# Down projections of a two-block transformer kernel: high and low activation parts moved as one 512-column matmul, the halves added at evacuation

## The chip, the core and the metric

The kernel runs on one NeuronCore of one Trainium2 chip. The metric is the device time of one execution in microseconds; the kernel before has a median of 1790.25 us over three runs.

## What is computed

256 tokens of width 1024 pass through two blocks. The first has a feed-forward network (FFN) before and after a token mixer; the second has two layers of the same shape. That makes six FFNs, numbered 0 to 5, and three mixers. Each FFN is

```
def swiglu(x, w_gate, w_up, w_down):
    return (jax.nn.silu(x @ w_gate) * (x @ w_up)) @ w_down
h = h + FFN_RES * g1[:, None, :] * swiglu(u, w_ff1_gate[l], w_ff1_up[l], w_ff1_down[l])
...
x = x + 0.5 * swiglu_2(rms_norm(x, ffn1_norm[l]), ffn1_w_in[l], ffn1_w_out[l])
```

with a hidden width of 2816. The change concerns `@ w_down` and the residual addition behind it, in all six FFNs.

## The kernel before

All activations lie transposed: features on the 128 partitions, the 256 tokens (`T`) in the free dimension, so the residual `h` is 8 tiles (`KD`) of 128x256 and the hidden activation 22 tiles (`KF`). Every large product is made in three float32r matmuls: weight and activation are each split into a high part (rounded to fp32r) and a low part (the rest), and high x high, high x low and low x high are accumulated (`three`, L1487 to L1491). ScalarE makes `whi` from the loaded weights `raw` (L717), VectorE makes `wlo` = raw - whi (L957). Weights come in chunks through a ring of 4 slots (`RING`): SyncE loads a slot when `lo_ready` says that VectorE has used it, ScalarE splits three chunks ahead (`HI_LEAD`), VectorE two chunks ahead (`LO_LEAD`), and TensorE counts `chunk_used`.

A down projection walks over m, the 8 output tiles. Each m has two chunks, an even one (t = 2m) with hidden tiles 0 to 10 and an odd one (t = 2m + 1) with hidden tiles 11 to 21. A chunk is 11 calls of `three`, which is 33 matmuls of 256 columns, each with a weight load of its own (a high weight tile is loaded twice, for its two matmuls). The sum lies in the first 256 columns of one of two PSUM banks (`acc`, "bank" in the profile), used in turn.

VectorE works through its part in a written order. `down(t)` for an even t is one weight split; for an odd t it is, in this order: wait for `chunk_used`; the evacuation L1121 (h = bank * gate + h, which signals `evacuated`); in FFNs 1 to 4 `gained_lo` (L986), which makes the low part of the next stage's input and waits for ScalarE's high part of the same tile (L743), which in turn waits for `evacuated`; and a weight split. FFNs 0 and 5 have no `gained_lo`. In FFN 0 VectorE also does two `ada_sum` steps per m (L1056: a modulation matrix, streamed in by GpSimd's queue, times the condition vector). GpSimd squares each finished tile of `h` for the next norm (L553, L554). VectorE, ScalarE and TensorE run most of a down projection in a hardware loop of two m per turn; VectorE's last turn is unrolled in FFNs 1 to 5, and all of it in FFN 0. The rows of `order` in the section on the change mark where an instruction waits.

Of the kernel before, what the change touches and what calls it, by code (L numbers as in the profile page):

```python
# [17 lines left out]
F32R = mybir.dt.float32r  # L18
U8 = mybir.dt.uint8
ALU = mybir.AluOpType  # L20
# [3 lines left out]
P = 128  # L24
T = 256
TT = T // P
D = 1024
KD = D // P
F = 2816
KF = F // P  # L30
# [130 lines left out]
def build(nc, a, out):  # L161
    with ExitStack() as ctx:
        ctx.enter_context(nc.allow_non_contiguous_dma(reason="two vectors of a few elements"))
        def sb(name, shape, dt=F32):
            return ctx.enter_context(nc.sbuf_tensor(name, shape, dt))

        def sem(name):
            return ctx.enter_context(nc.semaphore(name))
# [9 lines left out]
        wlo = sb("wlo", [P, RING, SLOT], F32R)  # L178
        h = sb("h", [P, KD, T])
        u = sb("u", [P, KD, T])  # L180
        uhi = sb("uhi", [P, KD, T], F32R)
        ulo = sb("ulo", [P, KD, T], F32R)
        work = sb("work", [P, 4, T])
        silu, hid = work[:, 0:2], work[:, 2:4]
        gate_up = work[:].rearrange("p (a b) t -> p a b t", a=2)
# [46 lines left out]
        qk_sq = toe  # L232

        hidden = ExitStack()
        hhi = hidden.enter_context(nc.sbuf_tensor("hhi", [P, KF, T], F32R))
        hlo = hidden.enter_context(nc.sbuf_tensor("hlo", [P, KF, T], F32R))
        hidden.close()
        lv = sb("lv", [P, TT, 512])
        place_of_aq_ak = ExitStack()
# [24 lines left out]
        acc = psum[0:2]  # L264
# [15 lines left out]
        evacuated = sem("evacuated")  # L280
        silu_ready = sem("silu_ready")
        hid_ready = sem("hid_ready")
        hhi_ready = sem("hhi_ready")
        hlo_ready = sem("hlo_ready")
        ada_landed = [sem(f"ada_landed{i}") for i in range(2)]
# [110 lines left out]
        def tiles_of(tile, m, it=0, per=0):  # L396

            if isinstance(it, int):
                return tile[:, m]
            return tile[:, bass.ds(it * per + m, 1)].rearrange("p a t -> p (a t)")  # L400
# [4 lines left out]
        def residual_gate(i):  # L405

            return [half[:, 0:8], half[:, 8:16]][i] if i < 2 else half8

        def seg(name):
            return FIRST[name], UNIT[name]  # L410
# [540 lines left out]
        def _(dve):  # L951
# [19 lines left out]
            def split_ahead(n, it=0):  # L971
                if n + LO_LEAD < len(COLS):
                    split_lo(n + LO_LEAD, it)
# [29 lines left out]
            def by_token(n):  # L1003
                return rstd[:, 0:T].unsqueeze(1).to_broadcast([P, n, T])
# [70 lines left out]
            def ffn(i):  # L1075
                n0, e0 = seg(f"up{i}")

                def step(t, it=0):
                    g = it * RING + KF * i + t + 1
                    ps = acc[(e0 + t) % 2]  # L1080
                    if i < 2:
                        dve.wait_ge(silu_ready, g)
                        nc.vector.tensor_tensor(hid[:, t % 2], silu[:, t % 2], ps[:, T:2 * T], ALU.mult  # L1083
                                                ).then_inc(evacuated, 1)
                        split_ahead(n0 + t, it)
                        if i == 0:
                            ada_sum(2 + t, it)
                    else:

                        pair = gate_up[:, t % 2]  # L1090
                        dve.wait_ge(chunk_used, it * RING + RING + n0 + t + 1)
                        nc.vector.tensor_tensor(pair, ps[:].rearrange("p (a t) -> p a t", a=2), by_token(2), ALU.mult  # L1092
                                                ).then_inc(evacuated, 1)
                        split_ahead(n0 + t, it)
                        dve.wait_ge(silu_ready, g)
                        nc.vector.tensor_tensor(pair[:, 1], pair[:, 0], pair[:, 1], ALU.mult).then_inc(hid_ready, 1)
                    dve.wait_ge(hhi_ready, g)
                    src = hid[:, t % 2] if i < 2 else gate_up[:, t % 2, 1]
                    nc.vector.tensor_tensor(tiles_of(hlo, t, it, RING), src, tiles_of(hhi, t, it, RING).bitcast(F32),  # L1099
                                            ALU.subtract).then_inc(hlo_ready, 1)  # L1100

                up_turns(dve, i, step)
                if i == 0:
                    dve.wait_ge(mod_taken, 1)
                    link(nc.vector.tensor_scalar(half[:, 0:8], mod[:, 2 * KD:3 * KD], 0.5, None, ALU.mult))
                n0, e0 = seg(f"down{i}")
                g = residual_gate(i)
                after = next_gain(f"down{i}")
                if i == 2:
                    final_residual()  # L1110

                def down(t, it=0):
                    if t % 2 == 0:
                        split_ahead(n0 + t, it)
                        if i == 0:
                            ada_sum(2 + KF + t, it)
                    else:
                        m = t // 2
                        dve.wait_ge(chunk_used, it * RING + RING + n0 + t + 1)
                        gm, hm = column(g, m, it, 2), tiles_of(h, m, it, 2)  # L1120
                        nc.vector.scalar_tensor_tensor(out=hm, in0=acc[(e0 + m) % 2][:, 0:T], scalar=gm, in1=hm,  # L1121
                                                       op0=ALU.mult, op1=ALU.add).then_inc(evacuated, 1)
                        if after is not None:
                            gained_lo(SPLITS.index(FOLLOWS[f"down{i}"]), after, m, it, 2)
                        split_ahead(n0 + t, it)
                        if i == 0:
                            ada_sum(2 + KF + t, it)


                turns = 2 * KD // RING - 1 if i else 0  # L1130
                if turns:
                    with dve.Fori(0, turns) as it:
                        for t in range(RING):
                            down(t, it)
                for t in range(turns * RING, 2 * KD):
                    down(t)
# [267 lines left out]
            ins = nc.vector.tensor_copy(vec_b[:, 0:B_ROWS], ps_score[:, P:P + B_ROWS])  # L1404
# [79 lines left out]
        def _(pe):  # L1484
            mm = nc.tensor.matmul

            def three(dst, wh, wl, xh, xl, first, last):  # L1487

                mm(dst, wh, xh, start=first, stop=False)  # L1489
                mm(dst, wh, xl, start=False, stop=False)  # L1490
                return mm(dst, wl, xh, start=False, stop=last)  # L1491

            def chunk_in(n, it=0):
                pe.wait_ge(lo_ready, it * RING + RING + n + 1)

# [62 lines left out]
            def ffn(i, stats=None):  # L1558

                n0, e0 = seg(f"up{i}")  # L1560
                waits = KD * SPLITS.index(f"up{i}")

                def step(t, it=0):
                    if i == 0 and t % KD == KD - 1:
                        group_sum(t // KD, it)
                    chunk_in(n0 + t, it)
                    bank_free(e0 + t, it, RING)
                    feature_tiles(n0 + t, acc[(e0 + t) % 2], range(2), 2 * P, KD, waits if t == 0 else None
                                  ).then_inc(chunk_used, 1)

                up_turns(pe, i, step, stats)
                n0, e0 = seg(f"down{i}")

                wide_ = 2 if i == 0 else 1
                with pe.Fori(0, 2 * KD // RING, wide_) as it:
                    for t in range(wide_ * RING):
                        if i == 0 and t == 1:
                            group_sum(2, it)
                        m, side = t // 2, t % 2
                        chunk_in(n0 + t, it)  # L1580
                        if side == 0:
                            bank_free(e0 + m, it, 2)
                        if t < 2:

                            pe.wait_ge(hlo_ready, KF * i + KF // 2 * (side + 1))
                        vh = kview(whi, (n0 + t) % RING, KF // 2, P)
                        vl = kview(wlo, (n0 + t) % RING, KF // 2, P)
                        for k in range(KF // 2):
                            kk = side * (KF // 2) + k
                            ins = three(acc[(e0 + m) % 2][:, 0:T], vh[:, k], vl[:, k], hhi[:, kk], hlo[:, kk],  # L1590
                                        kk == 0, kk == KF - 1)
                        ins.then_inc(chunk_used, 1)

            def level_column(hd, tt):
# [217 lines left out]
            for k in range(KD):  # L1812
                if k >= 2:
                    pe.wait_ge(x_taken, k - 1)
                for tt in range(TT):
                    at = k % 2 * 512 + tt * P
                    ins = nc.tensor.transpose(wide[:, at:at + P],
                                              xt[:, tt * D + k * P:tt * D + (k + 1) * P], ident)
# [8 lines left out]
            for half_ in range(2):  # L1827
                pe.wait_ge(early_step, KD - DIRECT + half_)
                for j in range(half_ * KD, (half_ + 1) * KD):
                    ins = mm(ps_mod[:, j:j + 1], early_sum[:, j * P:(j + 1) * P], ones[:, 0:1],  # L1830
                             start=False, stop=j == 2 * KD - 1)
# [16 lines left out]
            for c in range(TT * KD // 4):  # L1848
# [3 lines left out]
                for k in range(4):  # L1852
                    at = c % 2 * 512 + k * P
                    ins = nc.tensor.transpose(wide[:, at:at + P], h[:, k0 + k, tt * P:(tt + 1) * P], ident)
# [27 lines left out]
```

## Time and profile before

| | |
|---|---|
| median of 3 runs | 1790.25 us (1787.59 to 1791.26) |
| profiled execution, span from first to last instruction | 1789.7 us |
| TensorE matmul busy | 1704.9 us (95%) |
| VectorE busy | 1142.0 us (64%) |
| ScalarE, GpSimd busy | 775.7 us (43%), 322.4 us (18%) |
| mean granted TensorE clock | 0.983 of 2.4 GHz |

The span covers all but the launch; the profile gives no other time of its own for that execution, and 1789.7 us lies 0.55 us under the median. Busy shares are averages over stages with different limits. Matmuls are pipelined, so the duration of one (some 280 ns) is not what it costs in a row; the distance between two starts is.

### The profile page before, as it was taken

The page shows a single profiled execution, that of the slowest core. Times are in us where ns is not written, and L with a number is a line of the kernel's source. Part 1 is how long each engine was busy: PE and PEld are TensorE (multiplying, and loading weights), DVE is VectorE, ACT ScalarE, POOL GpSimd, SP SyncE. Part 2 cuts the span into 40 slices and gives each one's busy share as a digit, 9 for nine tenths or more (in the row PEclk, how much of TensorE's full clock was granted, in tenths as well). Part 3 has the DMA queues.
Part 4 walks back from the last instruction along what each step waited for, and adds up shares of the span by engine and source line. Part 5 has one row for each costly group of instructions (what it writes and reads, how often), then busy time and mean ns, then how long its engine had stood idle before and what let it go on. Part 6 is the DMA issues. An engine that isn't in the chain of part 4 may idle for free.

```text
span 1789.7 us, 34039 instructions
## 1 busy us (share of the span) xinstructions
PE 1704.9 (95%) x13692; PEld 1651.5 (92%) x13692; DVE 1142.0 (64%) x1317; ACT 775.7 (43%) x862; POOL 322.4 (18%) x363
## 2 busy tenths in 40 slices
PE   6999979999699999999999899999999999899998
PEld 6899978999699999999998799999999988799998
DVE  5666777667545566666587676656665577666654
ACT  1443333354344434543473345444544464355441
POOL 3200353500400053000143130001000134130000
PEclk9999989999899999999999999999999999999999
DMA  8987987435556557654733256557765643256653
GB/s 304 270 266 238 285 294 240 160 107 175 143 162 179 149 169 188 188 166 130 221 122 116 72 165 187 166 161 191 195 181 146 203 154 109 72 144 186 179 162 104
DMA packets 496971, 315.51 MB, mean 176 GB/s; under 512 B 14015, under 2 KB 487850, under 8 KB 495978
## 3 DMA queue, kind: packets, MB, share of 16 engines
q1 hardware_dynamic: 487604, 282.34, 54.7%
q0 software_dynamic: 8288, 30.15, 4.6%
q8 instruction: 71, 1.16, 0.3%
q10 hardware_dynamic: 982, 1.64, 0.3%
q14 instruction: 26, 0.21, 0.0%
HBM read 313.04 MB, written 1.05 MB: 175 GB/s over the span
## 4 chain that ended last, share of the span: by engine, by line
PE 78%; DVE 11%; ACT 4%; issue 3%; POOL 2%; DMA 1%; DVEq 0%; ACTq 0%; POOLq 0%
PE bank L1489 23%; PE bank L1491 22%; PE bank L1490 22%; DVE wlo L957 4%; PE wide L1617 1%; DVE wlo L966 1%; ACT uhi L743 1%; PE bank L1533 1%; DVE h L1121 1%; DVE ulo L986 1%; PE bank L1517 1%; ACT whi L717 1%; POOL u L670 1%; DMA in_turn<-in_w_ada 1%; PE bank L1519 1%
## 5 line engine op out<-in xcount | busy, mean ns | idle before, releaser
L1489 PE MATMUL bank<-uhi,whi 128*128 128x256 f32 x2752 | 789.2, 287 | 26.7 <-DVE ulo L980 16.8
L1490 PE MATMUL bank<-ulo,whi 128*128 128x256 f32 x2752 | 783.5, 285 | 0.0
L1491 PE MATMUL bank<-uhi,wlo 128*128 128x256 f32 x2752 | 783.2, 285 | 0.0
L1489 PEld LDWEIGHTS bank<-uhi,whi 128*128 128x128 f32 x2752 | 532.8, 194 | 34.6 <-issue 22.4
L717 ACT CAST whi<-raw 128x2048 fp32r<-128x2048 f32 (+2 forms) x294 | 499.4, 1701 | 150.2 <-PE bank L1491 115.9
L1490 PEld LDWEIGHTS bank<-ulo,whi 128*128 128x128 f32 x2752 | 533.2, 194 | 0.3 <-issue 0.2
L1491 PEld LDWEIGHTS bank<-uhi,wlo 128*128 128x128 f32 x2752 | 533.0, 194 | 0.0
L957 DVE TENSOR_TENSOR wlo<-raw,whi 128x2048 fp32r<-128x2048 f32 (+2 forms) x248 | 505.6, 2049 | 4.4 <-ACT gat L891 3.1
L1489 PE MATMUL bank<-hhi,whi 128*128 128x256 f32 x1056 | 301.4, 285 | 9.0 <-DVE wlo L957 9.0
L1491 PE MATMUL bank<-hhi,wlo 128*128 128x256 f32 x1056 | 298.6, 283 | 0.0
L1490 PE MATMUL bank<-hlo,whi 128*128 128x256 f32 x1056 | 298.5, 283 | 0.0
L1489 PEld LDWEIGHTS bank<-hhi,whi 128*128 128x128 f32 x1056 | 200.2, 190 | 13.5 <-DVE wlo L957 10.7
L1490 PEld LDWEIGHTS bank<-hlo,whi 128*128 128x128 f32 x1056 | 200.3, 190 | 0.0
L1491 PEld LDWEIGHTS bank<-hhi,wlo 128*128 128x128 f32 x1056 | 200.1, 189 | 0.0
L1092 DVE TENSOR_TENSOR work<-bank,rstd 128x512 f32<-128x512 f32 x88 | 60.9, 692 | 118.9 <-PE bank L1491 118.0
L769 ACT ACTIVATE work<-work 128x256 f32<-128x256 f32 x88 | 36.8, 418 | 215.2 <-DVE work L1092 215.2
L966 DVE TENSOR_TENSOR wlo<-raw,whi 128x1024 fp32r<-128x1024 f32 (+1 forms) x92 | 120.1, 1316 | 1.0 <-ACT whi L717 0.9
L551 POOL TENSOR_TENSOR sumsq<-h 128x256 f32<-128x256 f32 x9 | 8.0, 892 | 580.2 <-DVE h L1121 405.3
L1121 DVE SCALAR_TENSOR_TENSOR h<-bank,half,h 128x256 f32 (+1 forms) x48 | 23.2, 484 | 136.8 <-PE bank L1491 136.8
L1099 DVE TENSOR_TENSOR hlo<-work,hhi 128x256 f32 (+1 forms) x132 | 55.8, 423 | 55.8 <-ACT hhi L773 55.8
L553 POOL TENSOR_TENSOR sq<-h 128x256 f32<-128x256 f32 x63 | 57.8, 918 | 159.8 <-DVE h L1121 147.7
L1083 DVE TENSOR_TENSOR work<-work,bank 128x256 f32<-128x256 f32 x44 | 18.5, 421 | 102.0 <-ACT work L760 102.0
(276 smaller groups left out, 1814.2 us busy)
## 6 DMA issues: line engine op xcount, KB each, us to landing
raw<-in_ffn_w_in SPq DMA_DIRECT2D x176, 512.0 KB, 4.9
in_turn<-in_w_ada POOLq DMA_DIRECT2D x56, 512.0 KB, 5.6
raw<-in_w_mix_in SPq DMA_DIRECT2D x52, 512.0 KB, 4.5
raw<-in_ffn_w_out SPq DMA_DIRECT2D x64, 384.0 KB, 3.2
raw<-in_w_ff_gate SPq DMA_DIRECT2D x44, 512.0 KB, 4.0
raw<-in_w_ff_up SPq DMA_DIRECT2D x44, 512.0 KB, 5.2
raw<-in_w_in SPq DMA_DIRECT2D x40, 512.0 KB, 4.7
raw<-in_ffn_w_out SPq DMA_DIRECT2D x64, 320.0 KB, 3.8
```

What stands on the lines that cost most here:

```text
L553: link(nc.gpsimd.tensor_tensor(sq[:], h[:, k], h[:, k], ALU.mult))
L717: nc.scalar.copy(whi[:, n % RING, 0:cols], raw[:, n % RING, 0:cols]).then_inc(hi_ready, 1)
L769: nc.scalar.activation(pair[:, 0], pair[:, 0], ACT.Silu).then_inc(silu_ready, 1)
L957: nc.vector.tensor_tensor(wlo[:, n % RING, 0:cols], raw[:, n % RING, 0:cols], whi[:, n % RING, 0:cols].bitcast(F32), ALU.subtract).then_in ...
L966: ins = nc.vector.tensor_tensor(wlo[:, n % RING, c], raw[:, n % RING, c], whi[:, n % RING, c].bitcast(F32), ALU.subtract)
L1083: nc.vector.tensor_tensor(hid[:, t % 2], silu[:, t % 2], ps[:, T:2 * T], ALU.mult).then_inc(evacuated, 1)
L1092: nc.vector.tensor_tensor(pair, ps[:].rearrange("p (a t) -> p a t", a=2), by_token(2), ALU.mult).then_inc(evacuated, 1)
L1099: nc.vector.tensor_tensor(tiles_of(hlo, t, it, RING), src, tiles_of(hhi, t, it, RING).bitcast(F32), ALU.subtract).then_inc(hlo_ready, 1)
L1121: nc.vector.scalar_tensor_tensor(out=hm, in0=acc[(e0 + m) % 2][:, 0:T], scalar=gm, in1=hm, op0=ALU.mult, op1=ALU.add).then_inc(evacuated, 1)
L1489: mm(dst, wh, xh, start=first, stop=False)
L1490: mm(dst, wh, xl, start=False, stop=False)
L1491: return mm(dst, wl, xh, start=False, stop=last)
```

## The change

In the down projections only, the high and low parts of a hidden tile become one operand: `hhi` and `hlo` are now the two halves of one SBUF tensor `hid_parts` [128, 2, 22, 256]. `by_pairs` takes the place of `three`: one matmul of the high weight tile with 512 columns (256 of the high part, 256 of the low part) writes the whole bank, and one of the low weight tile with the 256 high columns adds to its first half. VectorE then reads both halves of the bank: it adds gate times the second half to `h`, waits for that instruction on a new semaphore `low_added`, and adds gate times the first half. `uhi` and `ulo` are put together as `u_parts` as well, but their matmuls stay as they were.

```diff
-        hhi = hidden.enter_context(nc.sbuf_tensor("hhi", [P, KF, T], F32R))
-        hlo = hidden.enter_context(nc.sbuf_tensor("hlo", [P, KF, T], F32R))
+        hid_parts = hidden.enter_context(nc.sbuf_tensor("hid_parts", [P, 2, KF, T], F32R))
+        hhi, hlo = hid_parts[:, 0], hid_parts[:, 1]
...
-                        nc.vector.scalar_tensor_tensor(out=hm, in0=acc[(e0 + m) % 2][:, 0:T], scalar=gm, in1=hm,
+                        ps = acc[(e0 + m) % 2]
+                        nc.vector.scalar_tensor_tensor(out=hm, in0=ps[:, T:2 * T], scalar=gm, in1=hm,
+                                                       op0=ALU.mult, op1=ALU.add).then_inc(low_added, 1)
+                        dve.wait_ge(low_added, it * 2 + KD * i + m + 1)
+                        nc.vector.scalar_tensor_tensor(out=hm, in0=ps[:, 0:T], scalar=gm, in1=hm,
                                                        op0=ALU.mult, op1=ALU.add).then_inc(evacuated, 1)
...
+            def by_pairs(dst, wh, wl, parts, first, last):
+
+                mm(dst[:, 0:2 * T], wh, parts, start=first, stop=False)
+                return mm(dst[:, 0:T], wl, parts[:, 0], start=False, stop=last)
...
-                            ins = three(acc[(e0 + m) % 2][:, 0:T], vh[:, k], vl[:, k], hhi[:, kk], hlo[:, kk],
-                                        kk == 0, kk == KF - 1)
+                            ins = by_pairs(acc[(e0 + m) % 2], vh[:, k], vl[:, k], hid_parts[:, :, kk],
+                                           kk == 0, kk == KF - 1)
```

TensorE's rows at the start of a down projection's loop in FFN 0 were these (whi and wlo are the weight parts, the last number the columns moved):

```order
L1497 ISA [waits lo_ready]
L1489 MATMUL bank<-hhi,whi 128x256 [waits hlo_ready,evacuated]
L1490 MATMUL bank<-hlo,whi 128x256
L1491 MATMUL bank<-hhi,wlo 128x256
L1489 MATMUL bank<-hhi,whi 128x256
L1490 MATMUL bank<-hlo,whi 128x256
```

and are now these:

```order
L1507 ISA [waits lo_ready]
L1500 MATMUL bank<-hid_parts,whi 128x512 [waits hlo_ready,evacuated]
L1501 MATMUL bank<-hid_parts,wlo 128x256
L1500 MATMUL bank<-hid_parts,whi 128x512
L1501 MATMUL bank<-hid_parts,wlo 128x256
```

Two instructions stand in the place of three; the waits stay at the same points.

VectorE's rows for one odd chunk and the even one behind it, in the loop of FFN 2's down projection, were:

```order
L1121 SCALAR_TENSOR_TENSOR h<-bank,half,h 128x256
L985 REGISTER_ALU
L986 ISA [waits uhi_ready]
L986 SCALAR_TENSOR_TENSOR ulo<-h,vec_b,uhi 128x256
L956 REGISTER_ALU
L957 TENSOR_TENSOR wlo<-raw,whi 128x1408 [waits hi_ready]
L956 REGISTER_ALU
L957 TENSOR_TENSOR wlo<-raw,whi 128x1408 [waits hi_ready]
```

and are now:

```order
L1123 SCALAR_TENSOR_TENSOR h<-bank,half,h 128x256
L1125 REGISTER_ALU
L1126 SCALAR_TENSOR_TENSOR h<-bank,half,h 128x256 [waits low_added]
L986 REGISTER_ALU
L987 ISA [waits uhi_ready]
L987 REGISTER_ALU
L987 SCALAR_TENSOR_TENSOR u_parts<-h,vec_b,u_parts 128x256
L957 REGISTER_ALU
L958 TENSOR_TENSOR wlo<-raw,whi 128x1408 [waits hi_ready]
L957 REGISTER_ALU
L958 TENSOR_TENSOR wlo<-raw,whi 128x1408 [waits hi_ready]
```

An evacuation with a wait on the one before it has come in ahead of everything that follows `evacuated`, and one register operation between the wait for `uhi_ready` and the instruction behind it.

## Rows read from the trace of the kernel before

**Rows 1.** The page: span, and busy time of each engine.
```profile
span 1789.7 us, 34039 instructions
...
PE 1704.9 (95%) x13692; PEld 1651.5 (92%) x13692; DVE 1142.0 (64%) x1317; ACT 775.7 (43%) x862; POOL 322.4 (18%) x363
```

**Rows 2.** The page: the chain that ended last, share of the span by line.
```profile
PE bank L1489 23%; PE bank L1491 22%; PE bank L1490 22%; DVE wlo L957 4%; PE wide L1617 1%; DVE wlo L966 1%; ACT uhi L743 1%; PE bank L1533 1%; DVE h L1121 1%; DVE ulo L986 1%; PE bank L1517 1%; ACT whi L717 1%; POOL u L670 1%; DMA in_turn<-in_w_ada 1%; PE bank L1519 1%
```

**Rows 3.** Timeline of VectorE, down projection of FFN 5: start us, us, instruction, [idle before].
```profile
1743.70 0.48 DVE L1121 SCALAR_TENSOR_TENSOR h<-bank,half,h 128x256 f32 x1 [4.27 <-PE bank L1491]
...
1751.54 0.48 DVE L1121 SCALAR_TENSOR_TENSOR h<-bank,half,h 128x256 f32 x1 [4.28 <-PE bank L1491]
```

**Rows 4.** Busy time by engine in 12 chunks of FFN 5's down projection.
```profile
1727.69:1774.68 46.99, 46.99 (x398) 46.99 (x397) 21.31 (x18) 15.12 (x11) 0.00 (x0) 1.00 0.53 145
```

**Rows 5.** Timeline of VectorE, down projection of FFN 4: loop, then unrolled turn.
```profile
1391.23 0.48 DVE L1121 SCALAR_TENSOR_TENSOR h<-bank,half,h 128x256 f32 x1 [2.89 <-PE bank L1491]
...
1424.29 0.48 DVE L1121 SCALAR_TENSOR_TENSOR h<-bank,half,h 128x256 f32<-128x256 f32 x1 [2.75 <-PE bank L1491]
...
1425.76 4.36 DVE L957 TENSOR_TENSOR wlo<-raw,whi 128x1408 fp32r<-128x1408 f32 x2
1432.19 0.48 DVE L1121 SCALAR_TENSOR_TENSOR h<-bank,half,h 128x256 f32<-128x256 f32 x1 [2.07 <-PE bank L1491]
```

**Rows 6.** The chain between two odd chunks there, in order of time: start us, us.
```profile
1399.53 0.49 DVE h L1121
...
1400.25 0.52 ACT uhi L743
...
1400.92 0.10 DVE ulo L986
...
1401.79 1.63 DVE wlo L957
...
1403.46 0.39 PE bank L1489
```

**Rows 7.** Timeline of VectorE, down projection of FFN 1.
```profile
641.19 0.48 DVE L1121 SCALAR_TENSOR_TENSOR h<-bank,half,h 128x256 f32 x1 [2.55 <-PE bank L1491]
...
649.93 0.48 DVE L1121 SCALAR_TENSOR_TENSOR h<-bank,half,h 128x256 f32 x1 [2.59 <-PE bank L1491]
```

**Rows 8.** Timeline of VectorE, FFN 0's down projection.
```profile
215.48 1.28 DVE L1056 SCALAR_TENSOR_TENSOR intra<-in_turn,c_act,intra 128x1024 f32<-128x1024 f32 x1 [0.45 <-DMA in_turn<-in_w_ada]
```

**Rows 9.** Busy time by engine there: clock, DMA share and GB/s stand last.
```profile
212.00:220.00 8.00, 8.00 (x70) 8.00 (x69) 6.20 (x6) 2.67 (x2) 4.05 (x4) 1.00 1.09 329
```

**Rows 10.** Timeline, weight loads of a row of one-column matmuls.
```profile
142.57 1.87 PEld L1525 LDWEIGHTS bank<-ones,intra 128*128 128x128 f32 x16
```

**Rows 11.** Timeline of TensorE: plain-float32 matmuls of 512 and 256 columns.
```profile
392.82 1.88 PE L1641 MATMUL wide<-xqk,ones 128*128 128x512 f32 x4
...
886.90 3.62 PE L1721 MATMUL ps_score<-h,wff 128*8 128x256 f32 x16 [0.58 <-DVE h L1121]
```

**Rows 12.** Timeline of TensorE at half clock, a down projection.
```profile
828.17 0.41 PE L1489 MATMUL bank<-hhi,whi 128*128 128x256 f32 x1
828.39 0.41 PE L1490 MATMUL bank<-hlo,whi 128*128 128x256 f32 x1
```

**Rows 13.** Timeline of VectorE: an instruction that waits for the one before it.
```profile
819.07 1.75 DVE L1024 RECIPROCAL toe<-toe 128x256 f32<-128x256 f32 x1
820.86 0.48 DVE L1026 SCALAR_TENSOR_TENSOR h<-h,vec_a,toe 128x256 f32<-128x256 f32 x1
```

**Rows 14.** The chain behind the last evacuation, FFN 0 and FFN 5.
```profile
251.24 0.50 DVE h L1121
...
251.87 2.53 POOL sq L553
...
1782.71 0.49 DVE h L1121
...
1783.26 0.67 PE wide L1854 x4
```

More of the change, by code:

```diff
@@ L180, in build @@
         u = sb("u", [P, KD, T])
-        uhi = sb("uhi", [P, KD, T], F32R)
-        ulo = sb("ulo", [P, KD, T], F32R)
+        u_parts = sb("u_parts", [P, 2, KD, T], F32R)
+        uhi, ulo = u_parts[:, 0], u_parts[:, 1]
         work = sb("work", [P, 4, T])
@@ L282, in build @@
         hid_ready = sem("hid_ready")
+        low_added = sem("low_added")
         hhi_ready = sem("hhi_ready")
```

## The prediction

> **What bounds the kernel now.** I read the page first. TensorE is busy 95% of the 1789.7 us span [rows 1], and its three split matmul lines make up 67% of the chain that ended last; but VectorE's weight split L957 stands on that chain too, with 4% [rows 2]. A busy share can't say where, so I read the six down projections apart, as the timeline of VectorE. The mark is the start of the evacuation L1121, once per output tile m, and the reader is to compare the distances. In FFN 5 it is 7.84 us, and VectorE sat idle for 4.28 us ahead of each [rows 3]: TensorE is the bound. Twelve chunks there, 396 matmuls, take 46.99 us (the 398 records of the window include two begun before it) [rows 4], so a 256-column matmul costs 118.7 ns from start to start, a chunk 3.92 us and an m 7.83 us.
>
> In FFN 4 the distance in the loop is 8.30 us (1391.23 to 1399.53) [rows 5, 6]. The chain shows what fills it: evacuation, ScalarE's high part (0.52 us), VectorE's low part, the weight split of 1.63 us, and only then TensorE's next odd chunk at 1403.46 [rows 6]. The period is 0.47 us over TensorE's own 7.83, which is TensorE's wait. A loop period there is thus a VectorE chain of 4.4 us plus one odd chunk of 3.9 us, and only the even chunk is hidden. FFNs 2 and 3 have the same order; in FFN 1 the period is 8.74 us [rows 7]. I count 21 such loop periods: 6 in FFN 1 and 5 in each of FFNs 2 to 4. The periods at the edge of these stages are near the balance: the unrolled one is 7.90 us, its split starts at 1425.76 and two splits take 4.36 us, so the first ends by about 1427.9, when TensorE needs it (1424.0 plus a chunk) [rows 5]. FFN 0 runs at TensorE's pace, but VectorE waits there for the modulation matrix (0.45 us once) [rows 8], with the DMA engines at a share of 1.09 and 329 GB/s [rows 9].
>
> **TensorE's part.** Per hidden tile three 256-column matmuls become one of 512 and one of 256. The trace of before has no 512-column fp32r matmul, so I bound it. What sets 118.7 ns? Sixteen loads with one-column matmuls, that is with no stream to speak of, start (1.87 - 0.19) / 15 = 112 ns apart [rows 10]: the load of a float32 tile is the longer part, as 256 columns at 2.4 GHz are 107 ns. Plain float32 matmuls give the stream alone: 512 columns start (1.88 - 0.59) / 3 = 430 ns apart, 256 columns (3.62 - 0.38) / 15 = 216 ns apart [rows 11], two column times for each column and only 3 ns over, their loads hidden. At half clock, 1.2 GHz, fp32r matmuls of 256 columns start 0.22 us apart, one column per cycle [rows 12]. Two column times of 256 columns are the stream of one fp32r matmul of 512: 216 ns. So I take 216 + 119 = 335 ns for a hidden tile, where 356 were: 21 ns, or s = 0.23 us per chunk. The bounds: nothing, if it is the reading of fp32r columns that takes 118.7 ns, since 512 then take 237; and 216 + 109 (107 and the same 2 to 3 over) = 325 ns, s = 0.34 us, if the small matmul runs at its stream too. I take the value near the load rows, because 112 without a stream explains most of 118.7.
>
> The Trainium skill (TensorE: Matmul & The Clock Gate, LDWEIGHTS) puts a load of 128 columns at about 107 ns. By it the 256-column matmul could run at its 109 ns and s would be 0.34 us; the loads that start 112 ns apart [rows 10] speak against the full amount.
>
> **VectorE's part.** The added evacuation has the shape of the one before it, 0.48 us [rows 5], and the second waits for the first: an instruction with such a wait started 1.79 us after one of 1.75 us [rows 13], so 0.04 us more. e = 0.52 us per m, ahead of `evacuated`. Behind it are queued ScalarE's high part, the low part, GpSimd's squares and the next weight split. Bounds: 0.48 if the wait costs nothing, 0.65 if the register operation for its value has to run between the two, as register operations do where ScalarE starts 0.23 us after the evacuation's end [rows 6]. I take 0.52, because the register operation stands ahead of the waiting instruction and can run during the first addition's 0.48 us.
>
> **The sum**, with s = 0.23 and e = 0.52:
> - 21 loop periods: the chain grows by e, only the odd chunk shrinks: 21 x 0.29 = +6.1 us.
> - Six edge periods (the unrolled one of FFNs 1 to 4, the first of 3 and 4), where the split comes up to 0.1 us early today: 6 x 0.25 = +1.5 us.
> - Chunks of these four stages ahead of their first evacuation, 7 with full effect (in FFN 2 one is held by other VectorE work): -1.6 us.
> - FFN 5: 16 chunks at TensorE's pace, VectorE's 0.48 + 0.52 + 3.2 us of work fits into 7.4 us: -3.7 us.
> - FFN 0: 16 chunks would be -3.7 us. But its modulation loads and weights would have to come 6% faster than the 329 GB/s with VectorE already waiting [rows 8, 9]. VectorE is in order, so a late load holds its next evacuation. Between 0 and 3.7 I take 2.0: -2.0 us.
> - The last evacuation of a stage is on the chain: in FFN 0 GpSimd's squares wait for it, in FFN 5 the output transposes [rows 14]; likewise ahead of the norms of FFNs 1, 2 and 4. In FFN 3 I expect the weight work of the next stage to cover it but for 0.1; without that cover it costs 0.52. +2.7 us.
> - The extra register operation ahead of the low part, once a turn in these stages, some 9 to 12 times: I take 0.04 us each, well under the 0.23 us of a hand-over with its register operations [rows 6]. +0.4 us.
>
> Joining `uhi` and `ulo` costs nothing: the up projections keep their matmuls. Together +3.4 us on the profiled 1789.7, so 1793.1; the median lies 0.55 us higher and the runs spread over 3.7, and I forecast 1793.2 us. A measurement of this kernel tells about 0.2%, 3.6 us, from no change.
>
> **Rivals.**
> 1. *The forecast: load-bound, gain and price nearly cancel.* s between 0.18 and 0.29. The sum holds s 50 times (66 with FFN 0 free of its DMA) and e some 32 times, so it ends between 1790 and 1797. For it: the loads 112 ns apart [rows 10] and the chain [rows 6]. Against: s rests on matmuls of another type. Chance 0.71.
> 2. *The stream is the bound, and TensorE gains nothing.* For it: 118.7 ns is above the 112 of the load alone. Against: plain float32 streams run 3 ns above their column time [rows 11]. s = 0 takes all gains away: 3.4 + 50 x 0.23 + 2.0 = +16.9 us, 1807. Chance 0.13.
> 3. *The other side: the small matmul sheds its excess too.* With s = 0.34 the sum is 3.4 - 50 x 0.11 = -2.1 us, and with FFN 0's DMA keeping up another 16 x 0.34 - 2.0 = 3.4 less: -5.5 us, 1784.7. The sign turns at s = 0.30 with FFN 0 held to 2.0 us, and at 0.26 with it free. For it: at 2.4 GHz 256 columns need only 107 ns. Against: the loads of 112 [rows 10] and the DMA share of 1.09 [rows 9]. Chance 0.12.
> 4. *Long matmuls overlap.* If 512 columns cost no more than 256, a hidden tile takes 237 ns and s is 1.3 us. FFN 5 saves 8 x 2.6 = 21 us, the 27 loop and edge periods 0.8 each = 21, the 7 early chunks 9, less 3 for the stage ends, FFN 0 some 2: about 1740. Against: at half clock 256 columns take 0.22 us, their full column time [rows 12]. Chance 0.02.
> 5. *The clock falls.* TensorE would idle over 1 us per period in FFN 1, where it now loses 8.74 - 7.83 = 0.9 [rows 7]. Each period of 8 us with 3 us at half clock would cost 1.5 us, six of them 9: 1802. Against: it kept full clock with 0.9. Chance 0.02.
>
> The Trainium skill (TensorE: Matmul & The Clock Gate, Back-to-back issue gap) states a sustained 131 ns for a 512-column matmul, which is close to the fourth rival. No row here shows a stream of more than one column per cycle, so the trace doesn't bear it out.
>
> **How the numbers follow.** The likeliest case gives 1793.2, close to the 1793.8 at which "slower by over 0.2%" begins: of its 0.71 I put 0.32 above. With rivals 2 and 5, slower has 0.47. Faster means under 1786.7: half of rival 3, rival 4, and 0.02 of the first for terms that I have mis-sized (the edges, FFN 0), 0.10. No change has the rest, 0.43. The range goes from 1787, where half of rival 3 is left out, to 1803, which takes in e = 0.65 (+4 us) and s down to some 0.1, and leaves out most of rival 2. The likeliest case alone is 1790 to 1797.
>
> **What would show it.** In the profile after, FFN 5's distance between evacuations should be 7.37 us, with matmul starts 216 and 119 ns apart; that of FFN 4's loop 8.6 us, with the weight split still last in the chain ahead of TensorE; FFN 1's 9.0; FFN 0 about 2 us shorter, with longer waits for the modulation DMA. The halves of an evacuation should start 0.52 us apart. The forecast is wrong if the 512-column matmul takes much other than 216 ns, if FFN 4's period shrinks, or if time moves in a stage without a down projection.

## The result: slower by 15 us, not by 3

The changed kernel takes 1805.17 us (median of 5 runs, 1800.41 to 1807.21), the kernel before, on the same chip, 1790.25 us (5 runs, 1787.17 to 1795.01). The ratio is 1.0084, with a 95% interval of 1.006 to 1.0108, which is 10.7 to 19.3 us slower. The forecast was 1793.2 us and its range ended at 1803. In the runs whose span is on record the time lies 1.7 us above the span, so the profiled execution of before (span 1789.7) took some 1791.4 us: about 1 us above the median, and not 0.55 us under it as the section on the time before has it.

The page of the changed kernel, span, busy times and the chain by line, answers to [rows 1, 2]:

```profile
span 1798.7 us, 32077 instructions
PE 1698.9 (94%) x12636; PEld 1595.3 (89%) x12636; DVE 1163.6 (65%) x1365; ACT 775.5 (43%) x862; POOL 319.3 (18%) x363
PE bank L1494 17%; PE bank L1496 17%; PE bank L1495 17%; PE bank L1500 9%; PE bank L1501 5%; DVE wlo L958 5%; PE wide L1627 1%; DVE wlo L967 1%; ACT u_parts L744 1%; DMA in_turn<-in_w_ada 1%; DVE h L1123 1%; DVE h L1126 1%; DVE u_parts L987 1%; PE bank L1543 1%; PE bank L1527 1%
```

TensorE has 1056 instructions fewer (12636, where 13692 were) and yet is busy only 6 us less; the weight split, now L958, has 5% of the chain, where L957 had 4% [rows 2].

Where TensorE saved is read first, from its timeline in a down projection at full clock (start us, us, instruction):

```profile
1190.04 0.39 PE L1500 MATMUL bank<-hid_parts,whi 128*128 128x512 f32 x1
1190.27 0.28 PE L1501 MATMUL bank<-hid_parts,wlo 128*128 128x256 f32 x1
1190.38 0.39 PE L1500 MATMUL bank<-hid_parts,whi 128*128 128x512 f32 x1
1190.61 0.28 PE L1501 MATMUL bank<-hid_parts,wlo 128*128 128x256 f32 x1
```

Read the distances of the starts, not the durations: the 512-column matmul takes 0.23 us to the next start (forecast 0.216), the 256-column one 0.11 to 0.12 (forecast 0.119). The timeline of VectorE in FFN 5, where TensorE is the bound, gives the pair more exactly:

```profile
1752.63 0.49 DVE L1123 SCALAR_TENSOR_TENSOR h<-bank,half,h 128x256 f32 x1 [3.65 <-PE bank L1501]
1753.15 0.48 DVE L1126 SCALAR_TENSOR_TENSOR h<-bank,half,h 128x256 f32 x1
1753.55 3.15 DVE L958 TENSOR_TENSOR wlo<-raw,whi 128x1408 fp32r<-128x1408 f32 x2
1760.35 0.48 DVE L1123 SCALAR_TENSOR_TENSOR h<-bank,half,h 128x256 f32 x1 [3.65 <-PE bank L1501]
```

1760.35 - 1752.63 = 7.72 us, where 7.83 were [rows 3, 4]. An output tile has 22 pairs, so a pair is 351 ns, where three matmuls took 356 (3 x 118.7). In that stage the 256-column one takes 120 ns of it, so the 512-column one takes 231. The saving is (7.83 - 7.72) / 2 = 0.055 us per chunk instead of 0.23. The halves start 0.52 us apart, as forecast.

In FFN 4 the same view, answering to [rows 5], shows the new loop period, 1415.18 - 1406.43 = 8.75 us, where 8.30 were:

```profile
1406.43 0.49 DVE L1123 SCALAR_TENSOR_TENSOR h<-bank,half,h 128x256 f32 x1 [2.81 <-PE bank L1501]
1406.95 0.48 DVE L1126 SCALAR_TENSOR_TENSOR h<-bank,half,h 128x256 f32 x1
1408.44 0.85 DVE L987 SCALAR_TENSOR_TENSOR u_parts<-h,vec_b,u_parts  x1 [1.00 <-ACT u_parts L744]
1409.21 3.15 DVE L958 TENSOR_TENSOR wlo<-raw,whi 128x1408 fp32r<-128x1408 f32 x2
1415.18 0.48 DVE L1123 SCALAR_TENSOR_TENSOR h<-bank,half,h 128x256 f32 x1 [2.81 <-PE bank L1501]
```

The chain there, answering to [rows 6], goes through the same work as before, with one more link (L1126):

```profile
1406.43 0.50 DVE h L1123
1406.95 0.49 DVE h L1126
...
1407.67 0.52 ACT u_parts L744
...
1408.44 0.10 DVE u_parts L987
...
1409.21 1.62 DVE wlo L958
...
1410.88 0.50 PE bank L1500
```

From the first half to TensorE's next odd chunk it is 1410.88 - 1406.43 = 4.45 us; it was 1403.46 - 1399.53 = 3.93 [rows 6]. The 0.52 us are there in full, and the odd chunk behind them gives back only 0.055. What TensorE waited in all for the split shows in the groups of its matmuls, idle time last. Of the kernel before:

```profile
L1489 PE MATMUL bank<-hhi,whi 128*128 128x256 f32 x1056 | 301.4, 285 | 9.0 <-DVE wlo L957 9.0
```

and of the changed one:

```profile
L1500 PE MATMUL bank<-hid_parts,whi 128*128 128x512 f32 x1056 | 375.2, 396 | 23.2 <-DVE wlo L958 23.2
```

So 14.2 us of waiting were added, while the 96 chunks together saved 96 x 0.055 = 5.3 us.

By stage, from the first to the last matmul start of each down projection in the trace, in us:

| | FFN 0 | FFN 1 | FFN 2 | FFN 3 | FFN 4 | FFN 5 |
|---|---|---|---|---|---|---|
| before | 66.1 | 67.6 | 70.6 | 65.1 | 65.0 | 62.5 |
| after | 65.5 | 70.4 | 70.5 | 68.1 | 68.2 | 61.7 |
| difference | -0.6 | +2.8 | 0.0 | +3.0 | +3.1 | -0.9 |

FFN 2 seems free, and is not. In the profile of before, TensorE's clock fell to half after its pause of 2.6 us there, and one chunk took 6.7 us; in that of the changed kernel, after a pause of 2.7 us, it did not, and the chunk took 4.0. The windows of that stretch show it (the clock is the third number from the end, 0.61 and 1.00). The pause ends at 826.1 us before and at 828.6 us after, so TensorE (the first busy time) has the more idle time in the second window. Before:

```profile
826.00:834.00 8.00, 7.91 (x43) 7.91 (x44) 3.91 (x4) 2.75 (x3) 0.61 (x1) 0.61 0.74 217
```

After:

```profile
826.00:834.00 8.00, 5.44 (x31) 4.76 (x32) 6.64 (x8) 1.78 (x2) 0.61 (x1) 1.00 0.34 96
```

A run of the changed kernel with nothing but another layout (the third experiment) had the fall in FFN 2 and took 73.1 us there: +2.6 on before. This is part of why the profiled spans differ by only 9.0 us (1798.7 and 1789.7); the profiled run of the changed kernel is also the fastest of its five. With the 2.6 us added back it is 11.6, inside the interval; the rest up to the medians' 14.9 lies in the spread of the runs, and I can't place it by a row.

### The profile page after: what moved, and what is told of

Its sections match the earlier page's. It is cut to its first block, busy times and chain, and to the rows that moved or that the text cites. A ratio compares the mean times of both kernels' runs of the same rounds, so it can differ in the third digit from the quotient of the medians.

```text
span 1798.7 us, 32077 instructions
## 1 busy us (share of the span) xinstructions
PE 1698.9 (94%) x12636; PEld 1595.3 (89%) x12636; DVE 1163.6 (65%) x1365; ACT 775.5 (43%) x862; POOL 319.3 (18%) x363
## 4 chain that ended last, share of the span: by engine, by line
PE 75%; DVE 13%; ACT 4%; issue 3%; POOL 3%; DMA 1%; DVEq 0%; ACTq 0%; POOLq 0%
PE bank L1494 17%; PE bank L1496 17%; PE bank L1495 17%; PE bank L1500 9%; PE bank L1501 5%; DVE wlo L958 5%; PE wide L1627 1%; DVE wlo L967 1%; ACT u_parts L744 1%; DMA in_turn<-in_w_ada 1%; DVE h L1123 1%; DVE h L1126 1%; DVE u_parts L987 1%; PE bank L1543 1%; PE bank L1527 1%
## 5 line engine op out<-in xcount | busy, mean ns | idle before, releaser
L1494 PE MATMUL bank<-u_parts,whi 128*128 128x256 f32 x2752 | 789.4, 287 | 25.6 <-DVE u_parts L981 16.8
L1495 PE MATMUL bank<-u_parts,whi 128*128 128x256 f32 x2752 | 783.3, 285 | 0.0
L1496 PE MATMUL bank<-u_parts,wlo 128*128 128x256 f32 x2752 | 783.0, 285 | 0.0
L1494 PEld LDWEIGHTS bank<-u_parts,whi 128*128 128x128 f32 x2752 | 532.8, 194 | 34.1 <-issue 21.5
L1495 PEld LDWEIGHTS bank<-u_parts,whi 128*128 128x128 f32 x2752 | 533.2, 194 | 0.3 <-issue 0.2
L1496 PEld LDWEIGHTS bank<-u_parts,wlo 128*128 128x128 f32 x2752 | 532.8, 194 | 0.0
L958 DVE TENSOR_TENSOR wlo<-raw,whi 128x2048 fp32r<-128x2048 f32 (+2 forms) x248 | 505.6, 2050 | 4.4 <-ACT gat L892 3.1
L1500 PE MATMUL bank<-hid_parts,whi 128*128 128x512 f32 x1056 | 375.2, 396 | 23.2 <-DVE wlo L958 23.2
L1501 PE MATMUL bank<-hid_parts,wlo 128*128 128x256 f32 x1056 | 298.2, 282 | 0.0
L1500 PEld LDWEIGHTS bank<-hid_parts,whi 128*128 128x128 f32 x1056 | 198.3, 188 | 76.5 <-DVE wlo L958 29.2
L1501 PEld LDWEIGHTS bank<-hid_parts,wlo 128*128 128x128 f32 x1056 | 198.6, 188 | 0.0
L1100 DVE TENSOR_TENSOR hid_parts<-work,hid_parts 128x256 f32 (+1 forms) x132 | 55.8, 423 | 61.1 <-ACT hid_parts L774 61.1
L744 ACT ACTIVATE u_parts<-h,vec_b 128x256 fp32r<-128x256 f32 (+1 forms) x40 | 19.5, 507 | 121.4 <-DVE h L1126 102.2
```

Of the source, the lines that this page charges most:

```text
L958: nc.vector.tensor_tensor(wlo[:, n % RING, 0:cols], raw[:, n % RING, 0:cols], whi[:, n % RING, 0:cols].bitcast(F32), ALU.subtract).then_in ...
L1500: mm(dst[:, 0:2 * T], wh, parts, start=first, stop=False)
L1501: return mm(dst[:, 0:T], wl, parts[:, 0], start=False, stop=last)
```

## The experiments

### One: the second evacuation alone

The kernel before, with an extra addition of the same shape (its factor zero) ahead of each evacuation.

```diff
+        low_added = sem("low_added")
...
+                        nc.vector.scalar_tensor_tensor(out=hm, in0=acc[(e0 + m) % 2][:, 0:T], scalar=zero8[:, 0:1], in1=hm,
+                                                       op0=ALU.mult, op1=ALU.add).then_inc(low_added, 1)
+                        dve.wait_ge(low_added, it * 2 + KD * i + m + 1)
                         nc.vector.scalar_tensor_tensor(out=hm, in0=acc[(e0 + m) % 2][:, 0:T], scalar=gm, in1=hm,
```

> The kernel before, with VectorE's part of the change alone: ahead of each evacuation stands an addition of 0 times the same 256 columns to h, and the evacuation waits for it on low_added. TensorE keeps its three 256-column matmuls. Theory A (VectorE's chain carries the price, TensorE's part gives almost nothing): the loop period of FFNs 2 to 4 goes from 8.30 to 8.82 us, FFN 1's from 8.74 to 9.26, FFN 5's stays at 7.84; in all 21 loop periods and the six edge periods and five stage ends by 0.52 or a little less, +14 to +17 us against before. Rival B (the price is not on VectorE, but in the new matmuls): under +6 us.

Measured: 1811.32 us (4 runs, 1807.36 to 1812.35) beside 1787.46 for the kernel before (18 runs); ratio 1.0108 (1.0076 to 1.014), which is 19 us, 14 to 25. The medians alone differ by 24 us, but the 18 runs of before spread over 10.5 us and their median lies near the lower end. The profiled spans differ by 16.0 (1805.7 and 1789.7), inside the 14 to 17 expected; the 19 lie above it. Timeline of VectorE, FFN 4:

```profile
1403.34 0.48 DVE L1122 SCALAR_TENSOR_TENSOR h<-bank,zero,h 128x256 f32 x1 [2.88 <-PE bank L1495]
1403.96 0.48 DVE L1125 SCALAR_TENSOR_TENSOR h<-bank,half,h 128x256 f32 x1
...
1412.24 0.48 DVE L1122 SCALAR_TENSOR_TENSOR h<-bank,zero,h 128x256 f32 x1 [2.87 <-PE bank L1495]
```

The period is 8.90 us, 0.60 over before; here the two additions start 0.62 us apart in the loop, 0.1 more than in the change, for a reason that no run shows; that makes this a slightly larger dose of it. FFN 5 keeps its 7.83. So the evacuation alone costs all that the change costs, and TensorE's part gave little back.

### Two: the wide matmul alone

The changed kernel without the addition of the low half and its wait.

```diff
-                        nc.vector.scalar_tensor_tensor(out=hm, in0=ps[:, T:2 * T], scalar=gm, in1=hm,
-                                                       op0=ALU.mult, op1=ALU.add).then_inc(low_added, 1)
-                        dve.wait_ge(low_added, it * 2 + KD * i + m + 1)
```

> The changed kernel without the first addition at the evacuation: the high weight tile times the low activation part is computed as in the changed kernel, but left out of the result. This is TensorE's part of the change alone. Theory A: a pair of matmuls costs 352 instead of 356 ns, 0.05 us per chunk, so -2 to -4 us against before, FFN 4's loop period 8.25 us. My prediction's size (0.23 us per chunk) would give -12 to -15 us. Rival B (new matmuls disturb others): slower than before.

Measured: 1784.35 us (10 runs, 1782.19 to 1787.86), ratio 0.9967 (0.9949 to 0.9984) to the same 18 runs: 6 us faster, 3 to 9, where 2 to 4 were expected. The medians differ by 3.1 us, the spans by 5.0 (1784.7 and 1789.7). FFN 4's period is 8.24:

```profile
1395.78 0.48 DVE L1123 SCALAR_TENSOR_TENSOR h<-bank,half,h 128x256 f32 x1 [2.82 <-PE bank L1498]
...
1404.02 0.48 DVE L1123 SCALAR_TENSOR_TENSOR h<-bank,half,h 128x256 f32 x1 [2.83 <-PE bank L1498]
```

That is 0.06 less than before, one odd chunk's saving. The gain is what a small s gives and not what my 0.23 would. The two parts add up within their intervals: +19 and -6 are +13 beside the +15 of both together, and by the profiled spans +16.0 and -5.0 are +11.0, beside 9.0 or, with the clock in FFN 2 alike, 11.6.

### Three: the halves side by side

The 512 moving columns come from two places 22 tiles apart. If the jump cost the 15 ns, columns that lie together would start 216 ns apart.

```diff
-        hid_parts = hidden.enter_context(nc.sbuf_tensor("hid_parts", [P, 2, KF, T], F32R))
-        hhi, hlo = hid_parts[:, 0], hid_parts[:, 1]
+        hid_parts = hidden.enter_context(nc.sbuf_tensor("hid_parts", [P, KF, 2, T], F32R))
+        hhi, hlo = hid_parts[:, :, 0], hid_parts[:, :, 1]
...
-                            ins = by_pairs(acc[(e0 + m) % 2], vh[:, k], vl[:, k], hid_parts[:, :, kk],
+                            ins = by_pairs(acc[(e0 + m) % 2], vh[:, k], vl[:, k], hid_parts[:, kk],
```

> The changed kernel with hid_parts laid out as [128, 22, 2, 256], so that the 512 columns of the wide matmul lie in a row instead of in two pieces 22 KB apart. Theory A (the fp32r stream itself, wherever it lies, takes more than its column time): starts stay at 233 and 120 ns, time within 0.2% of the changed kernel. Rival C (the jump between two pieces costs the missing 17 ns): the wide matmul takes 216 ns, FFN 5's distance of evacuations goes from 7.73 to about 7.36 us, and the time falls by 50 to 60 times 0.18 = 9 to 11 us, to about 1795.

Measured: 1804.88 us (9 runs, 1799.16 to 1807.71), ratio 1.0073 (1.0051 to 1.0095), the same as the change. TensorE's timeline in FFN 5:

```profile
1760.26 0.40 PE L1500 MATMUL bank<-hid_parts,whi 128*128 128x512 f32 x1
1760.50 0.28 PE L1501 MATMUL bank<-hid_parts,wlo 128*128 128x256 f32 x1
1760.62 0.40 PE L1500 MATMUL bank<-hid_parts,whi 128*128 128x512 f32 x1
```

Still 0.24 and 0.12. The layout plays no part. This run had the clock's fall in FFN 2, and shows the same pair at 1.2 GHz:

```profile
830.24 0.41 PE L1501 MATMUL bank<-hid_parts,wlo 128*128 128x256 f32 x1
830.45 0.63 PE L1500 MATMUL bank<-hid_parts,whi 128*128 128x512 f32 x1
830.88 0.41 PE L1501 MATMUL bank<-hid_parts,wlo 128*128 128x256 f32 x1
```

0.21 and 0.43 us, which is 256 and 512 columns at one per cycle of 1.2 GHz. What holds these matmuls back at 2.4 GHz doesn't show at 1.2.

### Four: half the weight columns

If the load of 128 weight columns were what takes 118.7 ns, 64 columns should take much less.

```diff
-                mm(dst[:, 0:2 * T], wh, parts, start=first, stop=False)
-                return mm(dst[:, 0:T], wl, parts[:, 0], start=False, stop=last)
+                mm(dst[0:64, 0:2 * T], wh[:, 0:64], parts, start=first, stop=False)
+                return mm(dst[0:64, 0:T], wl[:, 0:64], parts[:, 0], start=False, stop=last)
```

> The changed kernel with weight tiles of 64 columns in the down projections (half of each output tile is left out), so that a weight load takes half the time; streams stay at 512 and 256 columns. Theory A (the stream is the bound): 233 and 120 ns between starts as before. Rival D (the load, or its overlap with the stream, makes the excess): about 216 to 225 and 109 to 112 ns, FFN 5's period about 7.2 us instead of 7.73.

Measured: 1805.77 us, one run. TensorE's timeline in FFN 5 (128*64 are now the weights):

```profile
1760.57 0.39 PE L1500 MATMUL bank<-hid_parts,whi 128*64 128x512 f32 x1
1760.79 0.28 PE L1501 MATMUL bank<-hid_parts,wlo 128*64 128x256 f32 x1
1760.91 0.39 PE L1500 MATMUL bank<-hid_parts,whi 128*64 128x512 f32 x1
```

The starts are 0.22 to 0.23 and 0.12 us apart. FFN 5's distance is 7.62 us in this run (1750.86 to 1758.48), so a pair is 346 ns: half the weight columns take 5 ns off the two matmuls together, of the 26 by which 351 exceeds my 325. So a load of 112 ns is not what fills the 118.7, and the step "119 ns is mostly the load of 112" falls.

### Five and six: the weight split ahead of the wait

The remaining link of the theory is the place of the weight split: VectorE runs it behind the evacuation and the low part only because it is written there. In both kernels it was moved ahead of the wait for the chunk, in FFNs 1 to 5.

```diff
                         m = t // 2
+                        if i:
+                            split_ahead(n0 + t, it)
                         dve.wait_ge(chunk_used, it * RING + RING + n0 + t + 1)
...
-                        split_ahead(n0 + t, it)
                         if i == 0:
+                            split_ahead(n0 + t, it)
                             ada_sum(2 + KF + t, it)
```

In the kernel before:

> The kernel before, with one change of order on VectorE in the down projections of FFNs 1 to 5: for an odd chunk the weight split of the chunk after next is issued ahead of the wait for chunk_used and the evacuation, in the time in which VectorE sat idle, instead of behind the evacuation and the low part. Theory A (the loop periods over 7.83 us are the VectorE chain evacuation, ScalarE, low part, split): the periods of FFNs 1 to 4 fall to about 7.84 us, so 15 x 0.47 + 6 x 0.85 = 12 us less than before, 1775 to 1779. Rival E (another wait, ScalarE's high part of the weights or the DMA, is right behind): under 5 us.

In the changed kernel:

> The changed kernel with the same change of order. Theory A: with the split off the chain, the second evacuation has room in all stages and costs only 0.5 us at the stage ends (2.6 us in all); the matmul pair saves 96 x 0.05 = 4.6 us less what FFN 0 gives back. So within 3 us of the kernel before with that order, 1773 to 1778, and some 25 us under the changed kernel. Rival F (the price is the second evacuation's use of VectorE or PSUM, wherever it stands): over 8 us slower than the kernel before with that order.

Measured: before with the new order 1777.20 us (6 runs, 1774.85 to 1777.94), ratio 0.992 (0.9903 to 0.9936) to the kernel before in its old order, 1790.9 us (11 runs); changed with the new order 1775.07 us (6 runs, 1771.07 to 1780.32), ratio 0.9913 (0.9894 to 0.9933) to the same. The timeline of VectorE, FFN 4, first of before with the new order:

```profile
1372.27 0.48 DVE L1123 SCALAR_TENSOR_TENSOR h<-bank,half,h 128x256 f32 x1 [2.86 <-PE bank L1493]
...
1380.10 0.48 DVE L1123 SCALAR_TENSOR_TENSOR h<-bank,half,h 128x256 f32 x1 [2.42 <-PE bank L1493]
```

and of the changed kernel with it:

```profile
1376.42 0.49 DVE L1125 SCALAR_TENSOR_TENSOR h<-bank,half,h 128x256 f32 x1 [1.78 <-PE bank L1503]
...
1384.14 0.48 DVE L1125 SCALAR_TENSOR_TENSOR h<-bank,half,h 128x256 f32 x1 [1.79 <-PE bank L1503]
```

Both run at TensorE's own pace, 7.83 and 7.72 us. The groups of the last one's matmuls say the same, 2.7 us of waiting instead of 23.2:

```profile
L1502 PE MATMUL bank<-hid_parts,whi 128*128 128x512 f32 x1056 | 374.3, 396 | 2.7 <-DVE wlo L958 2.7
```

With the chain broken the second evacuation is hidden (VectorE is still idle 1.78 us a turn), and the change no longer costs anything: the intervals of the two overlap, and 2 us between the medians is less than they can tell. The one before gains 14 us by the order; the changed kernel gains some 30, though its 1805.17 and 1775.07 come from different sets of runs. Both beat both of the kernels compared here.

### Seven: operands of two bytes

If reading four-byte columns is what sets 231 and 119 ns, two-byte operands should meet their column times. All matmuls of the down projections take a tile of ones in bf16 for weights and moving columns.

```diff
+        half_word = sb("half_word", [P, 2 * T], mybir.dt.bfloat16)
...
+            nc.vector.memset(half_word[:], 1.0)
...
-                mm(dst[:, 0:2 * T], wh, parts, start=first, stop=False)
-                return mm(dst[:, 0:T], wl, parts[:, 0], start=False, stop=last)
+                mm(dst[:, 0:2 * T], half_word[:, 0:P], half_word[:], start=first, stop=False)
+                return mm(dst[:, 0:T], half_word[:, 0:P], half_word[:, 0:T], start=False, stop=last)
```

> The changed kernel, but the matmuls of the down projections read a bfloat16 tile of ones for weights and activations, in the same shapes (512 and 256 columns); the down products are left out of the result. Theory A1 (the stream of four-byte columns is limited by their reading): 216 and 109 ns between starts, the column time at 2.4 GHz and 2 to 3 ns. Rival A2 (the array itself, or the write to the bank, takes 233 and 120 for this shape): 229 to 233 and 118 to 120. Rival 4 of the prediction (long matmuls overlap): far less than 216.

Measured: 1787.9 us, one run. TensorE's timeline in FFN 5:

```profile
1760.41 0.27 PE L1503 MATMUL bank<-half_word 128*128 128x256 bf16 x1
1760.52 0.38 PE L1502 MATMUL bank<-half_word 128*128 128x512 bf16 x1
1760.73 0.27 PE L1503 MATMUL bank<-half_word 128*128 128x256 bf16 x1
1760.84 0.38 PE L1502 MATMUL bank<-half_word 128*128 128x512 bf16 x1
```

The starts are 0.11 and 0.21 to 0.22 us apart; a pair is (1760.84 - 1760.52) = 0.32 us. That is the pair of 325 ns that my third rival assumed, with a load ahead of every matmul. With that s and FFN 0 held by its DMA the prediction had 2.1 us less than before, and this run has 3.0 less than the 1790.9 beside it; but it is one run, the runs of before spread over 8 us, and the clock fell in FFN 0 here, so the closeness proves little.

The run changes three things at once: the moving columns, the weights, and the values, which are all ones. The weight loads became shorter too, as the pages of the changed kernel and of this run show (mean ns behind the comma):

```profile
L1500 PEld LDWEIGHTS bank<-hid_parts,whi 128*128 128x128 f32 x1056 | 198.3, 188 | 76.5 <-DVE wlo L958 29.2
L1502 PEld LDWEIGHTS bank<-half_word 128*128 128x128 bf16 x1056 | 104.1, 99 | 165.4 <-DVE wlo L959 38.4
```

With half the weight columns (the fourth experiment) the same figure is 135 ns, and the pair lost 5 ns; here it is 99, and the pair lost 26. That speaks for the operand type rather than the length of the load, but whether it is the moving columns or the weights whose four bytes cost the time is not shown, and the values are an untested rival.

### Eight: no accumulation

Another candidate is that adding to what a bank holds slows a 512-column matmul; here each one starts afresh.

```diff
-                mm(dst[:, 0:2 * T], wh, parts, start=first, stop=False)
-                return mm(dst[:, 0:T], wl, parts[:, 0], start=False, stop=last)
+                mm(dst[:, 0:2 * T], wh, parts, start=True, stop=True)
+                return mm(dst[:, 0:T], wl, parts[:, 0], start=True, stop=True)
```

> The changed kernel, but each matmul of the down projections starts a new sum (so all products but the last are left out of the result). Theory A1 (reading the moving operand is the limit): 233 and 120 ns as before. Rival G (adding to what the bank holds makes the excess): 216 and 109 ns.

Measured: 1810.52 us, one run, at a mean clock of 0.979. TensorE's timeline in FFN 5:

```profile
1760.27 0.39 PE L1500 MATMUL bank<-hid_parts,whi 128*128 128x512 f32 x1
1760.50 0.28 PE L1501 MATMUL bank<-hid_parts,wlo 128*128 128x256 f32 x1
1760.62 0.40 PE L1500 MATMUL bank<-hid_parts,whi 128*128 128x512 f32 x1
```

0.23 and 0.12 again. Accumulation plays no part.

## Why the prediction was wrong

**The step that failed is the size of s**, in the words of the prediction "Two column times of 256 columns are the stream of one fp32r matmul of 512: 216 ns. So I take 216 + 119 = 335 ns". The column time held, 427 ns at 1.2 GHz, but not at 2.4 GHz: there 512 fp32r columns take 231 ns on average (224 to 234 in most). Plain float32 [rows 11] looked like the same operand and was not a model for it: its rows run at two column times per column, so they say nothing on whether four-byte columns can pass at one per cycle. The half-clock rows [rows 12] were blind for the same reason. The row that had the answer was the one at hand: 118.7 ns for 256 columns is 0.464 ns each, and 512 of them are 237, nearer to the measured 231 than 216 is. That stood in the text as a bound, and I argued it away with the 112 ns of the load [rows 10], which the fourth experiment refutes: half the weight columns took 5 ns off a pair. Those rows, too, were loads for plain float32 matmuls and not for fp32r. A pair takes 0.351 us and s is 0.055.

**The sum with that s.** 3.4 + 50 x (0.23 - 0.055) = 12.2, and FFN 0 has -0.6 instead of the -2.0: 13.6 us, between the 11.6 by which the two profiles differ (with the clock in FFN 2 alike) and the 14.9 of the medians. The second rival (118.7 ns is what the 256 columns take, so TensorE gains nothing) was within 5 ns a pair of what was measured and, at 1807, had nearly the number; its argument against ("plain float32 streams run 3 ns above their column time") was the same mistake.

**Loop periods.** +0.52 - 0.055 on 8.30 gives 8.77; measured 8.75 in FFN 4. The price e was right to the hundredth, and so was the choice to let it lie whole on the chain of the loop periods.

**FFN 1.** Its period was forecast at 9.0 us, and is 9.08. That closeness is luck in part: with the measured s the same sum gives 8.74 + 0.465 = 9.2, and why the period is 0.1 us shorter is not shown.

```profile
641.09 0.48 DVE L1123 SCALAR_TENSOR_TENSOR h<-bank,half,h 128x256 f32 x1 [2.46 <-PE bank L1501]
...
650.17 0.49 DVE L1123 SCALAR_TENSOR_TENSOR h<-bank,half,h 128x256 f32 x1 [2.41 <-PE bank L1501]
```

TensorE idles 9.08 - 7.72 = 1.36 us a turn there and kept its clock, so the fifth rival did not come.

**FFN 0.** I gave it half of what 16 chunks could save, as DMA-bound. It saved 0.6 us of the 0.9 that s now allows. The prediction read one wait for the modulation matrix, of 0.45 us [rows 8]; the trace of before has four in this stage, 0.45, 0.91, 0.22 and 0.50 us. As forecast they have grown, from 2.1 us together to 3.4: 1.67, 0.47, 0.92 and 0.33, of which this is the first:

```profile
208.71 1.29 DVE L1057 SCALAR_TENSOR_TENSOR intra<-in_turn,c_act,intra 128x1024 f32<-128x1024 f32 x1 [1.67 <-DMA in_turn<-in_w_ada]
```

The two-byte run, whose chunks could save 16 x 0.34 = 5.4 us, can't be read here, since the clock fell to 0.50 in this stage. Where the DMA would have capped s = 0.23 stays open.

**Edges and ends.** The unrolled period of FFN 4, 7.90 us before [rows 5], is 1440.92 - 1432.57 = 8.35 us; the forecast had 0.25 for such a period with s = 0.23, which with the measured s is 0.43 where 0.45 came:

```profile
1432.57 0.48 DVE L1123 SCALAR_TENSOR_TENSOR h<-bank,half,h 128x256 f32<-128x256 f32 x1 [2.69 <-PE bank L1501]
...
1440.92 0.48 DVE L1123 SCALAR_TENSOR_TENSOR h<-bank,half,h 128x256 f32<-128x256 f32 x1 [2.00 <-PE bank L1501]
```

The last evacuation of a stage has its second half on the chain, 0.49 us and 0.03 of issue, behind FFN 0, as forecast. Outside the down projections the spans differ by 9.0 - 7.4 = 1.6 us. Of that, -0.5 lies ahead of FFN 0 and +2.1 behind the six stages, where 2.7 were forecast.

**The register operation.** It stands ahead of L987, and the idle time before that row is 1.00 us where the kernel before has 0.91 at L986: 0.09 us and not the 0.04 of the sum. But the split of the weights starts 0.77 us behind the start of the low part, where it was 0.87 (1401.79 - 1400.92 [rows 6]), so nothing of it is left on the chain, and the 0.4 us of the sum did not come.

**The other rivals.** The fourth (long matmuls overlap) is excluded by all timelines above: 512 columns never started less than 0.21 us apart. The 131 ns for a 512-column matmul that the Trainium skill (TensorE: Matmul & The Clock Gate, Back-to-back issue gap) states as sustained is not what this chip showed: in a stream with a load for each, 512 columns of two bytes took 0.21 to 0.22 us. The section's column time plus 2.5 ns, 216 and 109 ns, which it gives for single matmuls, is what these rows show, and the fp32r rows lie above it.

## What to carry to other kernels

When an instruction's cost has two candidate limits that lie within 6% of each other (here 112 ns of load and 118.7 ns measured), doubling one of them tells more than any argument; without that run, scale the row of the very operand type at the very clock, and treat a row of another type as the bound and not as the value. Price work on an engine by the place it has in the chain and not by its busy share: 0.5 us on VectorE, which is idle a third of the time, cost nearly its full amount on 27 turns because a weight split for the other engine was queued behind it, and cost nothing in the loops once that split was queued ahead of the wait. Joining two fp32r matmuls of 256 columns into one of 512 saved only 5 ns of 356 here.

## What the runs showed of the chip

- Matmuls with fp32r operands took 0.45 to 0.46 ns per moving column at 2.4 GHz (512 in 0.23 us, 256 in 0.12), and not the 0.417 ns of a column time, while at 1.2 GHz they met it (0.43 and 0.21 us). With bf16 operands they met it at 2.4 GHz (0.21 to 0.22 and 0.11 us). Layout and accumulation changed nothing here, and half the weight columns took 5 ns off a pair. Whether the moving columns, the weights or the values make the difference, and what inside the chip sets it, was not shown.
- In FFN 2, behind a pause of TensorE of 2.6 to 2.7 us, the clock fell in some executions (before, the third experiment) and not in others (after, the first experiment), which alone makes up to 2.7 us between two runs of one kernel.
